# Prompt attention of a hybrid decoder step: value products as four 32-query column tiles, and a new order of the tensor engine's step

## What is computed

```python
s = jnp.where(mask, q @ k.T * SCALE, -inf)
p = exp(s - max(s)) / sum           # masked_softmax, float32
o = p @ v                           # the value product
o_a = gates[..., 0:1] * o_cmp + gates[..., 1:2] * o_slc + gates[..., 2:3] * o_win
o_b = outs[g] * softmax(lses)[g]    # three dilated groups mixed
```

## Time and profile before

| | us |
|---|---|
| median of 3 runs | 1632.9 (1630.48 to 1633.38) |
| profiled execution, own time | 1625.36 |
| its span, first to last instruction | 1623.6 |
| prompt attention, first scores to last turn | 837.2 to 964.8 |
| TensorE busy over the span | 1532.9 (94%) |
| VectorE, ScalarE busy | 728.5, 557.5 |
| mean granted TensorE clock | 0.975 |

### The profile page before, as it was taken

The page is one execution under the profiler, slowest core; times in us unless marked ns, Lnnn a source line. Parts: engine busy times, 40 slices in busy tenths (PEclk is TensorE's granted clock), DMA queues, the critical chain, the costliest instruction groups (busy, mean ns, idle before and its releaser), DMA issues.

```text
span 1623.6 us, 26469 instructions
## 1 busy us (share of the span) xinstructions
PE 1532.9 (94%) x10935; PEld 1419.7 (87%) x10935; DVE 728.5 (45%) x1193; ACT 557.5 (34%) x898; POOL 169.3 (10%) x186
## 2 busy tenths in 40 slices
PE   2999999999999999999989989999789999999998
PEld 2788879999999999999766767787779999999998
DVE  4789975334323346266355442232564232223321
ACT  2443343222134322333435544544324332122211
POOL 4434200000000000000140013331000000000000
PEclk9999999999999999999879989999999999999999
DMA  8655413355344444232431018996122333223331
GB/s 237 235 183 182 150 32 130 129 170 159 121 159 142 150 143 135 105 108 76 130 103 32 1 64 231 258 266 186 40 66 78 87 103 90 70 85 96 87 106 56
DMA packets 194066, 202.16 MB, mean 125 GB/s; under 512 B 10774, under 2 KB 172381, under 8 KB 193437
## 3 DMA queue, kind: packets, MB, share of 16 engines
q1 hardware_dynamic: 171045, 111.64, 23.1%
q0 software_dynamic: 18592, 89.10, 16.7%
q10 hardware_dynamic: 4352, 0.34, 0.2%
HBM read 195.83 MB, written 31.40 MB: 140 GB/s over the span
## 4 chain that ended last, share of the span: by engine, by line
PE 90%; DVE 3%; ACT 2%; DMA 2%; issue 1%; POOL 1%; SPq 0%; DVEq 0%; ACTq 0%; POOLq 0%
PE PS L845 20%; PE PS L847 20%; PE PS L846 20%; PE PS L793 3%; PE PS L794 3%; PE PS L795 3%; PE PS L1137 3%; PE PS L1219 2%; PE PS L1101 2%; PE PS L1172 2%; PE PS L1195 1%; PE PS L1122 1%; PE PS L1200 1%; ACT DEC L1570 1%; PE PS L1237 1%
## 5 line engine op out<-in xcount | busy, mean ns | idle before, releaser
L845 PE MATMUL PS<-HNH,WHI 128*128 128x272 f32 x1408 | 408.7, 290 | 7.6 <-DVE HNL L1808 6.6
L846 PE MATMUL PS<-HNL,WHI 128*128 128x272 f32 x1408 | 406.8, 289 | 0.0
L847 PE MATMUL PS<-HNH,WLO 128*128 128x272 f32 x1408 | 406.3, 289 | 0.0
L845 PEld LDWEIGHTS PS<-HNH,WHI 128*128 128x128 f32 x1408 | 267.1, 190 | 10.4 <-issue 7.5
L846 PEld LDWEIGHTS PS<-HNL,WHI 128*128 128x128 f32 x1408 | 267.7, 190 | 0.0
L847 PEld LDWEIGHTS PS<-HNH,WLO 128*128 128x128 f32 x1408 | 267.6, 190 | 0.0
L1713 DVE TENSOR_TENSOR WLO<-WR,WHI 128x1024 fp32r<-128x1024 f32 (+3 forms) x144 | 192.3, 1342 | 153.3 <-ACT WHI L1344 152.7
L1344 ACT ACTIVATE WHI<-WR 128x1024 fp32r<-128x1024 f32 (+3 forms) x144 | 164.7, 1152 | 274.1 <-DMA WR<-in_ffn_in 125.5
L845 PE MATMUL PS<-HIDH,WHI 128*128 128x272 f32 x704 | 202.4, 288 | 0.0
L847 PE MATMUL PS<-HIDH,WLO 128*128 128x272 f32 x704 | 202.4, 287 | 0.0
L846 PE MATMUL PS<-HIDL,WHI 128*128 128x272 f32 x704 | 202.0, 287 | 0.0
(11 more groups left out here) (368 smaller groups left out, 2424.4 us busy)
## 6 DMA issues: line engine op xcount, KB each, us to landing
WR<-in_ffn_in SPq DMA_DIRECT2D x88, 512.0 KB, 3.6
WR<-in_ffn_out SPq DMA_DIRECT2D x32, 704.0 KB, 4.4
out_dil_s<-in_cache_dil_kv POOLq DMA_DIRECT2D x8, 2044.0 KB, 9.2
WR<-in_w_in SPq DMA_DIRECT2D x14, 648.0 KB, 4.2
BIG<-in_cache_dil_kv SPq DMA_DIRECT2D x8, 512.0 KB
WR<-in_w_out SPq DMA_DIRECT2D x8, 512.0 KB, 4.5
out_dil_s<-in_cache_dil_kv POOLq DMA_DIRECT2D x8, 508.0 KB, 5.1
out_win_s<-in_cache_win_kv POOLq DMA_DIRECT2D x8, 508.0 KB, 5.2
```

The lines of the kernel that those rows point to most:

```text
L845: pe.matmul(out, a[0], b[0], start=first, stop=False)
L846: pe.matmul(out, a[0], b[1], start=False, stop=False)
L847: return pe.matmul(out, a[1], b[0], start=False, stop=last)
```

## The change

Four things change. Each value product is cut into four products of 32 queries, whose results go to four quarters of the PSUM partitions. The compressed probabilities and values are held on 128 partitions in place of 31, with zeros below, so that their product has the same shape as the others; VectorE clears them once before the stage. The order within a step of the tensor engine changes: both turns, then both value products of the entry before, then the scores of entry `e+2`. The semaphores, the other engines' order and all transfers stay.

```diff
-        CVPO = WR[0:31, o + 2800:o + 2930].rearrange("p (h c) -> p h c", h=2)
+        CVPO = WR[:, o + 2800:o + 2930].rearrange("p (h c) -> p h c", h=2)
...
-        PCT = CVf[0:31, 0:768].rearrange("p (h n) -> p h n", h=2)
+        PCT = CVf[:, 0:768].rearrange("p (h n) -> p h n", h=2)
...
                 if E["k"] in (1, 3, 5):
-                    pe.matmul(out[:, h, 0, :], PCT[:, h, E["q"] * P:(E["q"] + 1) * P], CVPO[:, h, :], start=True, stop=True)
+                    for z in range(0, P, 32):
+                        pe.matmul(out[z:z + 32, h, 0, :], PCT[:, h, E["q"] * P + z:E["q"] * P + z + 32], CVPO[:, h, :],
+                                  start=True, stop=True)
                 for y in range(n):
-                    mm = pe.matmul(out[:, h, E["b"], :], PTS[:, E["a"] % 2, h, y * P:(y + 1) * P],
-                                   VV[:, E["j0"] + y, E["v"] + h, :], start=(y == 0), stop=(y == n - 1))
+                    for z in range(0, P, 32):
+                        mm = pe.matmul(out[z:z + 32, h, E["b"], :], PTS[:, E["a"] % 2, h, y * P + z:y * P + z + 32],
+                                       VV[:, E["j0"] + y, E["v"] + h, :], start=(y == 0), stop=(y == n - 1))
                 mm.then_inc(pa[f"pv{h}"], 1)
...
                 turn(e, 0)
+                turn(e, 1)
                 if e:
+                    values(e - 1, 0)
                     values(e - 1, 1)
-                turn(e, 1)
                 if e + 2 < NE:
                     scores(e + 2)
-                values(e, 0)
+            values(NE - 1, 0)
             values(NE - 1, 1)
...
-                    act.activation(PCT[:, h, :], PS[0:31, 4 + h, 0:384], ACT.Copy).then_inc(pa[f"ev{h}"], 1)
+                    act.activation(PCT[0:31, h, :], PS[0:31, 4 + h, 0:384], ACT.Copy).then_inc(pa[f"ev{h}"], 1)
...
-            V.memset(CVPO[:, :, HD:HD + 1], 1.0)
+            V.memset(CVPO, 0.0)
...
             V.tensor_tensor(OA, PS[:, 6, 0:192].rearrange("p (b r) -> p b r", b=NB), GW[:, :, 0, :], ALU.mult)
+            V.memset(PCT, 0.0)
             dve.wait_ge(sc["turn"], 1)
...
-            V.tensor_copy(CVPO[:, :, 0:HD], PS[0:31, 3, 2 * HD:4 * HD].rearrange("p (h d) -> p h d", h=2))
+            V.memset(CVPO[0:31, :, HD:HD + 1], 1.0)
+            V.tensor_copy(CVPO[0:31, :, 0:HD], PS[0:31, 3, 2 * HD:4 * HD].rearrange("p (h d) -> p h d", h=2))
```

## The result

The kernel after took 1615.7 us (median of 4 runs, 1614.7 to 1616.3) beside 1631.7 for the kernel before (4 runs, 1630.5 to 1633.4): ratio 0.990, 95% interval 0.988 to 0.991. Forecast were 1627.4, with 1622 as the low end. Faster was right; the gain is 16 us where 5.5 were forecast.

What follows compares the result with a forecast made beforehand. TensorE was taken as the bound (90% of the chain); its work falls 20.7 us, but a two-step loop through other engines leaves -6.8, taken as -5.5: 1632.9 - 5.5 = 1627.4 us, range 1622 to 1647.

Steps and rivals of the forecast that it cites:

- Pace of the tiles: Value products on TensorE: four column tiles load and multiply beside each other, 0.0565 us a pass, 0.113 a product against 0.226.
- Rivals A: Value products: tiles share loads or multiplies, so a pass stays at 0.113 us; 1633 to 1642 us; chance 2 in 10.
- B: Value products: instruction issue is the bound, 0.063 us by product or pair; 1639 to 1647 or 1690 us; chance 2 in 10.
- Shape change of the compressed product: Compressed products on 31 rows: the array empties twice, 0.45 us each beyond their multiplies; 24 make 10.8 us removed.
- The loop: Prompt attention, n=4: combine, lowest score, ScalarE, turn and value products close over two steps in 7.38 us, 3.69 a step.
- TensorE's own sum: Step at n=4: TensorE's turns, products, scores, masks and shape changes add to 3.34 us, less than the loop's 3.69.
- Query tile by query tile: Prompt attention stage: -5.2 us at n=4, -2.6 at n=3, +0.5 each at n=2 and n=1, total -6.8.
- the losses at n=1 and n=2: First two query tiles: the two-step loop binds, costing 0.5 us in each.
- what I allowed for seams: Between query tiles: waits that remain, with the clock stretch, cut the gain from 6.8 to 5.5 us.
- the sum's last one: Whole kernel: the 5.5 us gain is set against the median, 1632.9 - 5.5 = 1627.4, though the profiled execution was 7.5 below it.
- Rival C: TensorE with more gaps may be granted 1.2 GHz longer, up to 3.4 us per stretch; 1627 to 1637; chance 1 in 10.
- The parts at nothing: Clearing PCT (0.7 us) and CVPO falls into VectorE waits; transfers, PSUM copies and work after the stage add nothing.

Runs made afterwards that it cites:

- e11: Changed kernel with the loop over the four column tiles outermost, so products of one tile follow one another; 1630.4 us, ratio 0.999.
- e15: Changed kernel with whole 128-query products, where each product after the first of an entry moves 33 columns instead of 65; 1629.7 us.
- e1: Kernel before with only the new order of the step; whole products, compressed product on 31 rows; 1645.6 us, ratio 1.009.
- e3: Changed kernel without column tiles: new order, compressed product on 128 rows, whole 128-query products; 1635.2 us, ratio 1.003.
- e9: Kernel before with only the compressed product changed from 31 rows to 128; old order, whole products; 1622.5 us, ratio 0.9945.
- e5: Changed kernel with VectorE's lowest score of entry e+2 moved ahead of the combine of entry e-1; 1606.9 us, ratio 0.985.
- e6: Changed kernel with both ScalarE copies of an entry moved ahead of the next entry's exponentials; 1605.7 us, ratio 0.985.
- e0: Kernel before, unchanged, profiled a second time; 1632.4 us.
- e13: Changed kernel with the old order for entries 0 to 9 (n=1) and the new order from entry 10 on; 1622.5 us, ratio 0.994.
- e12: Changed kernel with the new order only for entries 0 to 9 (n=1), the old order for the rest; 1616.9 us, ratio 0.991.

## Why the prediction was right or wrong

**Pace of the tiles: right, by a reason that was only half right.** Forecast 0.0565 us for a pass, measured 0.0567. Rivals A (0.113) and B (0.063 a pair) are out: a pair starts every 0.0142 us. But I split the whole product's 0.113 into two halves for load and multiply, and e11 and e15 show that it can't be split so: 0.0565 for 65 columns was right by luck.

The Trainium skill, TensorE: Matmul & The Clock Gate, "Wait — 56ns, not 53.3ns?", gives a floor of 25 ns from start to start of multiplies; the 14.2 ns here, over four column tiles, are below it. The Trainium skill, TensorEngine Tiling (Array Packing), Key Properties, says that tiles load and multiply in parallel; the 0.0142 of four tiles in turn against the 0.0352 of one tile agree, though four tiles gain 2.5 times, not 4.

**Shape change of the compressed product: right, a little short** (0.22 forecast; 0.34 between e1 and e3, 0.3 in e9).

**The loop: right in place, long by 4%.** Forecast 7.38 us, measured 937.31 - 930.21 = 7.10 from one combine's start to the next's. I added up durations; ScalarE's four instructions take 2.26 us from 933.17 to 935.43 where I had 2.68, since the next starts some 0.1 before the last has ended; the turn, the products and VectorE's start behind them took 0.2 longer than forecast. e5 and e6 show that this loop decides. TensorE's own sum of 3.34 a step was right too: in e6, where it decides, the steps at n=4 average 3.2.

**Query tile by query tile.** At full clock n=4 fell 47.0 to 41.6, forecast 5.2; n=3 32.4 to 29.4, forecast 2.6. n=1 and n=2 don't lose 0.5 each: with 6.8 us at 1.2 GHz the first tile takes 18.7 before and 18.8 after; and where (26.9 - 18.7) / (26.9 - 6.8) = 0.41 us are taken off for each us at 1.2 GHz, n=2 is 24.9 to 25.8 before, 24.8 to 25.0 after. So the work is worth 5.4 + 3.0 + some 0.5, about 9 us, where I summed 6.8 and took 5.5: the losses at n=1 and n=2 and what I allowed for seams are not in the figures. The executions say the same: the 13 of the kernel before at 0.974 or more have a median of 1624.7, 9.0 above the changed kernel's.

**The step that failed is the sum's last one.** "I take the difference and set it against the median": that holds only if both kernels stand as far above their profiles. The 7.5 us between the profiled execution and the median were the clock of the first query tile (26.9 us long and all of it at 1.2 GHz, where the profile behind the forecast had 18.7 us with 6.8 of them at 1.2 GHz), and the changed kernel has it in neither of its two profiles, nor, to go by their times, in any of its ten executions with a clock shown (1612.8 to 1618.3 at 0.973 to 0.980). So about 9 us of the 16 are work of the tiles from n=2 up, and some 7 the clock at n=1. Rival C had the clock right as a mechanism and looked only to one side of it; the low end, 1622, had no case in it where the clock gives time back. What rival C feared is small: the 6.8 us at 1.2 GHz at n=3 in the first profile of the changed kernel cost 3.2 (32.6 against 29.4), near the 3.4 of the prediction. With the 9 us of work in place of 5.5 the forecast would have been 1623.9, with the 7.5 us in place of nothing 1619.9; the clock is the larger error of the two. The parts at nothing (the clearing, the stage after) were right.

**Why the new order looked harmless.** It costs with whole products on 31 rows (e1), is worth 1.4 us with tiles at n=3 and n=4, and its main gift is the clock at n=1. How it brings that about is open. In the windows of e0 and e13, TensorE is busy for 26.1 and 26.2 of 27 us, in e12 for 21.9, but these gaps come behind the rise of the clock and not ahead of it. Two profiles of the same kernel, the first one of before and then e0:

```profile
838.00:842.00 4.00, 3.63 (x23) 2.41 (x24) 1.30 (x4) 1.70 (x6) 2.80 (x4) 0.50 0.89 245
842.00:846.00 4.00, 4.00 (x26) 2.74 (x26) 1.05 (x3) 2.06 (x7) 1.79 (x2) 0.75 1.06 273
```

```profile
838.00:842.00 4.00, 3.63 (x20) 2.28 (x20) 1.36 (x4) 2.04 (x6) 3.09 (x4) 0.50 1.04 291
842.00:846.00 4.00, 4.00 (x19) 2.89 (x18) 0.43 (x1) 1.77 (x7) 0.49 (x1) 0.50 1.03 291
```

TensorE is busy for 3.63 and 4.00 us in both, and the clock rises in the one and not in the other. So it is in e12 and e13: busy for 4.00 of 4 us from 842 to 846 and again from 846 to 850, where e12's clock is 0.88 and e13's 0.50. An experiment with more idle time and nothing else changed in the first tile wasn't made.

## What to carry to other kernels

Before a forecast is set against a median, ask where the profiled execution and the median part, by the granted clock stage by stage and, where there is one, a second profile of the same kernel: here that difference was half the answer. An operation that brings an odd shape of the array between others (31 rows among 128) is worth padding by itself: 9 us for one edit (e9). When TensorE's work shrinks, look at once for the loop that closes through the other engines, and try their order too: moving ScalarE's copies ahead of its exponentials gave another 10 us.

## What was not expected of the hardware

Multiplies with 65 float32 columns start 0.0142 us apart over four column tiles, 0.0296 over two and 0.0352 in one, where a whole product's start 0.108 to 0.113 apart with 65 columns and 0.106 with 33 in three of four. And the same program has 27 or 7 us at 1.2 GHz in its first query tile from one profiled execution to the next; by their mean clocks alone, for none of these was profiled, 57 of 70 further executions were of the first kind and 13 of the second.
